# The head of the first pass in another order: loads, turns, high parts and two column pairs

## The reference, cut to what matters

```python
for layer in range(DEPTH):
    h = rmsnorm(x, attn_norm_g[layer])
    proj = h @ w_in[layer]
    gm_u, gm_v, ssm_z, ssm_xbc, ssm_dt, da_q, da_k, da_v, gates = split_cols(proj, IN_SIZES)
    ...
    # in the mixer: xbc = silu(causal_dwconv(ssm_xbc, conv_w, conv_b)), 1536 channels, 4 taps
    # xs, bm, cm = split_cols(xbc, (1024, 256, 256)); dt = softplus(dt_raw + dt_bias); a scan follows
```

## Time and profile before

| | |
|---|---|
| median of 3 executions | 1811.37 us (1810.8 to 1811.43) |
| the profiled execution | 1810.55 us, span of its instructions 1808.5 us |
| busy share of the span | TensorE 99%, VectorE 77%, ScalarE 58%, GpSimd 1% |
| first slice of 40 (45 us each) | TensorE 8 tenths, VectorE 7, DMA 9 |
| mean DMA rate | 181 GB/s, 234 in the first slice |

### The profile page before, as it was taken

The page is one execution under the profiler, slowest core; times in us unless marked ns, Lnnn a source line. Parts: engine busy times, 40 slices in busy tenths (PEclk is TensorE's granted clock), DMA queues, the critical chain, the costliest instruction groups (busy, mean ns, idle before and its releaser), DMA issues.

```text
span 1808.5 us, 26087 instructions
## 1 busy us (share of the span) xinstructions
PE 1797.2 (99%) x10250; PEld 1570.3 (87%) x10250; DVE 1385.1 (77%) x2040; ACT 1045.6 (58%) x1287; POOL 18.7 (1%) x45
## 2 busy tenths in 40 slices
PE   8999999999999999999999999999999999999998
PEld 8898889888989888888889888898889888889887
DVE  7968887997697887799868756679957765578974
ACT  6667646775565774577645456555544456556543
POOL 1000000000000000000000000000000000000000
PEclk9999999999999999999999999999999999999999
DMA  9977556655988665555556565555556565555553
GB/s 234 202 160 158 176 179 194 201 189 188 180 163 162 161 176 181 169 186 187 198 179 194 177 192 183 182 169 191 191 178 197 179 195 187 174 180 185 192 180 105
DMA packets 254962, 328.01 MB, mean 181 GB/s; under 512 B 25909, under 2 KB 169537, under 8 KB 254841
## 3 DMA queue, kind: packets, MB, share of 16 engines
q1 hardware_dynamic: 254576, 326.00, 61.2%
q10 hardware_dynamic: 264, 0.35, 0.1%
HBM read 325.23 MB, written 1.09 MB: 180 GB/s over the span
## 4 chain that ended last, share of the span: by engine, by line
PE 95%; DVE 2%; DVEq 1%; DMA 0%; issue 0%; ACT 0%; SPq 0%; ACTq 0%
PE psum L715 19%; PE psum L656 15%; PE psum L658 15%; PE psum L657 15%; PE psum L724 10%; PE psum L644 10%; PE psum L752 4%; DVEq L1572 1%; PE psum L854 1%; DVE xbc L1693 0%; DMA x<-in_x 0%; PE psum L936 0%; PE psum L1088 0%; PE psum L1068 0%; PE psum L1075 0%
## 5 line engine op out<-in xcount | busy, mean ns | idle before, releaser
L424 ACT ACTIVATE w_hi<-w_raw 128x2048 fp32r<-128x2048 f32 (+2 forms) x309 | 574.3, 1859 | 284.7 <-PE psum L658 248.1
L412 DVE TENSOR_TENSOR w_low<-w_raw,w_hi 128x1024 fp32r<-128x1024 f32 (+1 forms) x310 | 375.6, 1212 | 233.2 <-ACT w_hi L424 225.7
L656 PE MATMUL psum<-w_hi,act 128*128 128x512 f32 x1248 | 492.3, 394 | 0.2 <-DVE w_low L416 0.2
L658 PE MATMUL psum<-w_hi,act 128*128 128x512 f32 x1248 | 486.4, 390 | 0.0
L657 PE MATMUL psum<-w_low,act 128*128 128x512 f32 x1248 | 486.1, 389 | 0.0
L715 PE MATMUL psum<-act,w_hi 128*128 128x512 f32 x1536 | 366.5, 391 | 0.0
L416 DVE TENSOR_TENSOR w_low<-w_raw,w_hi 128x1024 fp32r<-128x1024 f32 (+2 forms) x307 | 360.9, 1176 | 0.0
L715 PEld LDWEIGHTS psum<-act,w_hi 128*128 128x128 f32 x1536 | 282.3, 188 | 54.7
L658 PEld LDWEIGHTS psum<-w_hi,act 128*128 128x128 f32 x1248 | 234.3, 188 | 49.7
L656 PEld LDWEIGHTS psum<-w_hi,act 128*128 128x128 f32 x1248 | 234.5, 188 | 47.4 <-DVE w_low L416 0.6
L657 PEld LDWEIGHTS psum<-w_low,act 128*128 128x128 f32 x1248 | 234.6, 188 | 46.2
(11 more groups left out here) (285 smaller groups left out, 1573.1 us busy)
## 6 DMA issues: line engine op xcount, KB each, us to landing
w_raw<-in_w_in SPq DMA_DIRECT2D x121, 1024.0 KB, 6.0
w_raw<-in_ffn_w_up SPq DMA_DIRECT2D x40, 1024.0 KB, 5.1
w_raw<-in_w_up SPq DMA_DIRECT2D x40, 1024.0 KB, 5.1
w_raw<-in_ffn_w_down SPq DMA_DIRECT2D x16, 1024.0 KB, 5.0
w_raw<-in_w_down SPq DMA_DIRECT2D x16, 1024.0 KB, 5.0
w_raw<-in_w_branch_b SPq DMA_DIRECT2D x8, 1024.0 KB, 5.1
w_raw<-in_w_out SPq DMA_DIRECT2D x8, 1024.0 KB, 5.1
w_raw<-in_w_a SPq DMA_DIRECT2D x8, 1024.0 KB, 5.4
```

The costliest lines, as they stand in the source:

```text
L412: dve.tensor_tensor(lo[:, 0:cut, :], of[:, 0:cut, :], hi[:, 0:cut, :], ALU.subtract).then_inc(w_lo_front, 1)
L424: act.activation(group_view(whi, q % HIGH, g), group_view(raw, q % LOW, g), ACT.Copy).then_inc(w_hi, 1)
L656: mm(o, xh, hi[:, k, :], start=g["opens"] and k == 0, stop=False)
L658: last = mm(o, xl, hi[:, k, :], start=False, stop=g["closes"] > 0 and k == g["kt"] - 1)
```

## The change

SyncE issues x's right half ahead of the back half of the first weight group. ScalarE squares that half between the front and back high part of group 0, takes the root behind the scaled copies of the right half, and makes both halves of XBC2's high part ahead of the third and fourth normed pair. VectorE's part is written out as `first_norm`: the mean square ahead of the back low part of group 0, and the normed pairs interleaved with the splits as the other norms have it. TensorE makes 9 of the 14 warming products first and 5 behind the bias product, and spreads 1/root behind the front high products of group 1. In both layers the fifth and the sixth column pair of XBC change places, in the load, the convolution's tiles and parameters and the silu.

```diff
+XBC_PAIR = (0, 1, 2, 3, 5, 4)
...
-                return of("w_in", 0, D, dict(GU=0, Z=1024, XBC=2048)[kind] + 256 * n)
+                return of("w_in", 0, D, dict(GU=0, Z=1024, XBC=2048)[kind] + 256 * (XBC_PAIR[n] if kind == "XBC" else n))
...
-            first_load(0)
+            first_front(0)
             x_half(1)
-            first_load(1)
-            first_load(2)
+            first_back(0)
+            for q in (1, 2):
+                first_front(q)
+                first_back(q)
...
                     early_products(q, G, a0, (0, 1), False)
+                    if q:
+                        spread_rest()
                     pe.wait_ge(w_lo_front, plain_count(1, 0, q + 1))
...
-                    if q == 0:
-                        spread_rest()
...
-            for n in range(14):
-                mm(PJ[:, BANKS[0], 0:P], ones[:, :], ones[:, :], start=True, stop=True)
+            keep_clock(9)
             pe.wait_ge(ident_in, 32)
             turn(1, 0, 0, 0)
             pe.wait_ge(step("bias_const_in"), 48)
             mm(bias_bank, qkv[0:32, 0:12], qkv[0:32, 512:1024], start=True, stop=True).then_inc(step("bias_product"), 1)
+            keep_clock(5)
...
-            first_high(0)
+            front_high(0)
             x_squares(1, 0, 0, 1)
+            back_high(0)
             for i in range(LAYERS):
-                norm_root(1, i, 0)
+                if i:
+                    norm_root(1, i, 0)
                 xg_high(1, i, 0, 2)
                 xg_high(1, i, 0, 3)
                 if i == 0:
-                    first_high(1)
+                    norm_root(1, i, 0)
+                    front_high(1)
+                    back_high(1)
                     norm_high(1, i, 0, A_H, range(0, 2))
                     front_high(at_group(1, 0, 2))
+                    back_high(at_group(1, 0, 2))
                     norm_high(1, i, 0, A_H, range(2, PAIRS))
-                    back_high(at_group(1, 0, 2))
...
-                    v = xbc[:, 2 * n:2 * n + 2, :]
+                    v = xbc[:, 2 * XBC_PAIR[n]:2 * XBC_PAIR[n] + 2, :]
...
+            def first_norm():
+
+                front_low(0)
+                bias_rows()
+                mean_square(1, 0, 0)
+                back_low(0)
+                xg_low(1, 0, 0, 2)
+                xg_low(1, 0, 0, 3)
+                rstd_of("root", 1, rstd, "rstd_ready")
+                front_low(1)
+                back_low(1)
+                norm_rstd(1)
+                normed(1, 0, 0)
+                normed(1, 0, 1)
+                for p in range(PAIRS):
+                    split_low("h_hi", p + 1, slice(A_H + 2 * p, A_H + 2 * p + 2), h32[:, 2 * p:2 * p + 2, :], "h_ready")
+                    if p + 2 < PAIRS:
+                        normed(1, 0, p + 2)
+                low_part(V, at_group(1, 0, 2))
```

51 lines of the change are left out of this document (22 added, 29 removed).

## The result

The changed kernel takes 1816.73 us (median of 12 runs, 1811.78 to 1820.62) against 1811.36 us before (12 runs in turn with them, 1810.78 to 1811.61). The ratio is 1.0029, 95% interval 1.0021 to 1.0036: slower, by 5.4 us, where 0.4 us less than before was forecast. Its 12 runs spread over 9 us, the 12 of the kernel before over 0.8.

The account below looks back on a forecast made before the run. TensorE was taken as the bound, with VectorE second in the head; the parts summed 0 + 0 + 0 + 0 + 0 − 0.4 = −0.4 us, giving 1810.15 profiled, 1811.0 median, range 1809.6 to 1812.9.

Parts of the forecast that it names:

- The parts forecast at zero: Head: load order, rstd spread, squares and root, warming products, and interleaving were each worth 0 in the sum.
- the pairs' 20.34: VectorE in the head: the copy of rstd and the normed pairs start at 20.34, as before.
- The sign named for it: Clock rival, 0.05: TensorE's warming passes never reach 11 per us before 6.3; about 1.7 us lost, 1813.0 us.
- that lead: TensorE at XBC2: first product at about 23.65 instead of 24.30; worth 0.65 to 1.1 us for TensorE, 0 for VectorE.
- The second layer was worth 0: Second layer: TensorE is busy 2.00 of 2.00 us during the slow load, so the exchange moves nothing there.
- The chain that carries XBC5's landing: From XBC5's landing L through ScalarE's high part and GpSimd to VectorE's low half, ending at L + 5.57.
- The low half at 37.40: VectorE, beside GpSimd: shrinks from 2.88 to 1.22 us with the pairs exchanged, giving VectorE a lead of 1.66 us.
- XBC4 did not wait: TensorE's 0.66 us wait at 36.77 goes; XBC4 starts at 35.7, a lead of 1.1 us.
- The step that failed: Head loads after the exchange: XBC4's lands at 30.6, XBC5's (L) at 39.6, leaving a lead of 0.35 us.
- The slow load hurts more where it goes: Rival, 0.09: XBC5's load lands beyond 39.94; hard form L = 44.8, 4.9 us lost, 1816.3; milder form 1812.9.
- 39.94: VectorE's remaining lead at XBC5's low half is 39.94 − L, at most 1.66 us; a later landing loses one for one.

Follow-up runs that it names:

- after_no_pair: The changed kernel with the column pairs of XBC in their old order, all other edits kept: 1811.47 us, ratio 1.0000 (0.9991 to 1.0009).
- after_second_only: The changed kernel with the pair exchange kept in the second layer alone, the first layer in the old order: 1811.53 us, ratio 1.0002.
- before_dt_early: The kernel before, nothing exchanged, with the 64 KB step weights issued ahead of the load of columns 3072, not behind it: 1814.88 us, ratio 1.0019.
- only_pair: The kernel before with one edit, the exchange of the fifth and sixth column pair of XBC: 1815.96 us, ratio 1.0025 (1.0015 to 1.0035).
- after_dt_early: The changed kernel with the step weights issued ahead of both exchanged loads: median 1812.05 us; seven of ten runs 1810.19 to 1812.69, three 1815.07 to 1816.13.
- before_dt_late: The kernel before with the step weights issued behind XBC5's load: 1811.98 us, ratio 0.9995 to 1.0014.
- after_dt_late: The changed kernel with the step weights issued behind both exchanged loads, no longer between them: 1812.77 us, ratio 1.0011 (1.0002 to 1.0020).
- slow_third: The changed kernel with columns 3072 taken as the third pair and XBC2's own columns as the fifth: 1814.51 us, ratio 1.0018 (1.0009 to 1.0027).

## Why the prediction was wrong

**The parts forecast at zero came to nothing in the time.** The order of x and the first weights, the spread, the squares and the root, the warming products and the interleaving are together in `after_no_pair`: 1811.47 us. On VectorE one of the zeros was 0.5 us: the copy of rstd came at 20.37 and the normed pairs at 20.86, against 19.84 and 20.34 before (the forecast gives the pairs' 20.34 for both). The back half of the second group had landed at 18.12 and not at 17.58. The clock had risen ahead of x's turn with nine warming products as with fourteen: its eight passes took 1.09 us, 1.04 before. In this trace it fell only behind XBC3's wait. The sign named for it, 11 passes in the us before 6.3, could not show, since the nine products ended at 5.55. (Of the 6 and 11 passes read from the earlier trace rows 4 and 9 start in their microsecond, the others reach into it; the ratio is about one to two either way.) XBC2's first product came at 24.23 and not 23.65, so most of that lead did not appear; it was worth nothing either way. The second layer was worth 0, as `after_second_only` shows.

**The chain that carries XBC5's landing was right for this execution.** The step said that the low half of XBC5 ends at L + 5.57 when GpSimd holds it up. With the measured L of 44.12 that is 49.69, and it ended at 49.60; in `before_dt_early` L = 45.15 gives 50.72, and it ended at 50.64. In the five other late traces GpSimd did not hold it up, and it ended 2.1 to 2.4 us sooner than that (49.13 and not 51.26 in `only_pair`). They are as slow all the same, by the landing of QK2, a path that the prediction does not have. The low half at 37.40 did shrink from 2.88 to 1.23 us (39.53 above), and XBC4 did not wait. The Trainium skill (SBUF — State Buffer, section "SBUF: two separate sides") gives an exclusive lock that the first of the two takes for its whole instruction; the trace agrees in the 1.08 us of both, and in XBC3's halves, where VectorE started 0.05 us ahead (32.49 against 32.54) and GpSimd's took 3.43. In `only_pair` it does not fit: GpSimd is recorded 0.23 us ahead and is still the one held up, though recorded starts on GpSimd are rough.

**The step that failed** is the one that set the landings: "With the pairs exchanged the load for XBC4 should land at 26.0 + 4.6 = 30.6", "If the two loads only trade places, L stays 39.4", "so I take L = 39.6". The loads did not trade places. XBC3's load, which the change does not touch and which I left at 26.0, landed at 30.48; XBC4's at 33.20; XBC5's at 44.12. The rival "The slow load hurts more where it goes", to which I gave 0.09, named the right place, L = 44.8 and 1816.3 us. That its numbers are so near is luck. It put 14.2 us behind a landing of XBC4 at 30.6; measured are 10.9 us behind 33.20. And the columns 3072 are not slow alone, 8.9 us against 6.9 to 10.6 for others.

**What led me there** was one sentence: "That this is a matter of the columns and not of the small load of dt's weights behind it is shown by the second layer". A low rate in the second layer at XBC4's load shows that the small load is not needed for a slow stretch. It doesn't show that the small load costs nothing. The exchange moved it relative to the columns 3072, from behind them to ahead of them, and the diff shows nothing of this, since its own line stays put. Moving it back gave 4.0 of 5.4 us; moving it alone, with no exchange, cost 3.65 us (1814.88 against 1811.23 in the same runs).

**What the runs show in its place.** Two landings are late, and they occur apart. One: XBC5's load lands at 42.8 to 45.8 in all seven kernels of the table that have the step weights ahead of the columns 3072, and at 38.9 to 41.2 in the seven others, the changed order among them. QK2's is late with it: 58.79 to 62.88 in the first seven, 54.05 to 57.49 in the others. Two: XBC3's load lands at 28.8 to 32.5 in all eight kernels whose next column load is 3328, and at 25.5 to 26.7 in all six where it is 3072. With XBC5's late and XBC3's on time the median is 1814.9 us (one kernel, in which XBC4's is late as well). With XBC3's alone it is 1812.8 (1815.1 where XBC3's wait was nearly twice as long), with both 1816.0 to 1817.4, `after_dt_early` apart. How a landing becomes time differs from trace to trace, by VectorE's low half or by QK2 and the silus; the start of the first `xbc` product sums it up, 4.2 to 7.3 us later than before in the seven late ones.

**What stays open.** Why XBC3's load is late when 3328 is behind it: it isn't when the loads run alone (there it landed 21.8 to 24.4 us behind the first issue in the new order, 21.8 to 23.8 in the old one). Why the pieces of 64 bytes cost only in that place in the kernel, and in both orders when the loads run alone. And why `after_dt_early` mostly escapes. What the engines do during the loads, or when each load is released, may take part, since these are differences left between the kernel and the loads alone; neither was tried apart. The pieces themselves were no longer in flight in the changed kernel's slow stretch: the step weights landed at 33.65, and the low rate lasted to 42. Nor was it tried to take the high part of QK2 out of the silus' way. No version here beats the kernel before; `after_no_pair` (1811.47) ties with it.

## What to carry to other kernels

An order of loads in one queue can't be priced by exchanging the durations seen in the old order: the load in front and the loads behind move too, and a small load that stays in its line of the code has changed its neighbours. Where the landing of one load decides, as in a head that VectorE and TensorE run through without slack, try the exchange alone and the small load's place alone before anything is built on them. And a wait that is gone from the profile (0.66 us at XBC4) says little while the next load's landing is a guess: write down for each load by how much it may be late before its reader is, here 0.5 us at XBC5 (39.94 against 39.4). Do it for the loads behind as well: a high part that waits for its load holds up all that stands behind it on ScalarE, and QK2's, which the prediction does not name, is what TensorE waited for last in six of the seven traces with a late XBC5.

## What the chip showed that I had not expected

- 64 KB in pieces of 64 bytes among 8 MB of loads cost 4.0 to 7.5 us with nothing else running; 64 KB in pieces of 512 bytes, ahead of the columns 3072 in the kernel, cost nothing measurable (1811.86 against 1811.59 us).
- One megabyte alone took 6.9 to 10.6 us by columns of the same matrix, and four in a row 22.5 to 22.6 us in one order and 24.4 to 25.3 in two others.
- The DMA engines were 97 to 105% busy at 68 to 88 GB/s from 38 to 42 us, and 102% busy at 364 GB/s from 44 to 46 us. In this kernel their busy share says nothing of the rate.
- TensorE's clock fell to half in or behind waits of 1.93, 3.91 and 3.10 us in the head, for 3.4, 6.8 and 6.8 us. It did not fall in `after_dt_late`, behind a wait of 2.23 us. It also fell for 3.4 us within 10 to 16 us in `before_dt_late` and 12 to 16 in `slow_third`, ahead of the loads that this is about.
- Where GpSimd and VectorE made the low halves of one group within 0.5 us of each other, one of the two took 3.0 to 3.7 us and not 1.2 or 2.4, and it can be either: VectorE's in the changed kernel (3.03), GpSimd's in `only_pair` (3.70).
- The wide spread of the changed kernel (9 us over 12 runs) does not follow from the exchange alone: `only_pair` stayed within 0.8 us over 8 runs, and the kernel before, at 0.8 us over 12 runs in the result, spread over 2.1 to 3.0 us beside the experiments.
